# FFN gate and up products of a two-block kernel by Strassen's scheme, with summed weights kept in device memory

## The reference

```
def swiglu(h, w_gate, w_up, w_down):
    return (jax.nn.silu(h @ w_gate) * (h @ w_up)) @ w_down

# in first_block; D_FF is 2816
x_lat = x_lat + m_lat[2][:, None] * rms_norm(y_lat, norm_mix_post[layer])
f_lat = swiglu(modulate(rms_norm(x_lat, norm_ffn_pre[layer]), m_lat[3], m_lat[4]),
               w_gate[layer], w_up[layer], w_down[layer])
x_lat = x_lat + m_lat[5][:, None] * rms_norm(f_lat, norm_ffn_post[layer])
```

## Time and profile before

| | us |
|---|---|
| median of 3 runs | 3360.96 |
| lowest and highest | 3360.37, 3362.12 |
| time of the profiled execution | 3361.19 |
| its span in the profile | 3359.4 |
| PE busy (x instructions) | 3256.7 (x18179) |
| DVE, ACT, POOL busy | 1660.1, 1321.2, 252.8 |
| mean granted clock of PE | 0.988 |
| DMA | 328.24 MB, 98 GB/s in the mean |

### The profile page before, as it was taken

The page is one execution under the profiler, slowest core; times in us unless marked ns, Lnnn a source line. Parts: engine busy times, 40 slices in busy tenths (PEclk is TensorE's granted clock), DMA queues, the critical chain, the costliest instruction groups (busy, mean ns, idle before and its releaser), DMA issues.

```text
span 3359.4 us, 43733 instructions
## 1 busy us (share of the span) xinstructions
PE 3256.7 (97%) x18179; PEld 2585.9 (77%) x18179; DVE 1660.1 (49%) x2404; ACT 1321.2 (39%) x2266; POOL 252.8 (8%) x302
## 2 busy tenths in 40 slices
PE   6899888899999999999999999999999999999999
PEld 6677656787878878889955579999999555688887
DVE  6767576554343443345454553444434545534433
ACT  4532455454232333234445543333334455423322
POOL 1000313400000000000120000000000300000001
PEclk8999989999999999999999999999999999999999
DMA  6545213133333334333200112442432001124323
GB/s 246 167 156 164 82 44 114 58 127 112 120 115 96 97 94 170 94 94 118 88 1 7 51 48 89 132 131 85 149 128 85 6 7 51 47 88 134 108 94 113
DMA packets 97749, 328.24 MB, mean 98 GB/s; under 512 B 11456, under 2 KB 12880, under 8 KB 96784
## 3 DMA queue, kind: packets, MB, share of 16 engines
q1 hardware_dynamic: 77120, 252.55, 23.5%
q0 software_dynamic: 18896, 68.63, 5.9%
q10 hardware_dynamic: 1536, 4.26, 0.3%
HBM read 299.19 MB, written 26.21 MB: 97 GB/s over the span
## 4 chain that ended last, share of the span: by engine, by line
PE 90%; DVE 5%; ACT 2%; DMA 1%; issue 1%; ACTq 0%; DVEq 0%; POOL 0%; POOLq 0%
PE psum L146 88%; DVE mixer L175 2%; PE psum L149 2%; DVE mixer L185 1%; DVE wlo L175 1%; DMA mixer<-in_wm 1%; DVE junk L189 1%; DMA stage<-in_wi 0%; ACT whi L163 0%; DMA hold<-in_wq 0%; ACT arena L154 0%; ACT mixer L154 0%; ACT mixer L155 0%; DVE mixer L180 0%; ACT mixer L163 0%
## 5 line engine op out<-in xcount | busy, mean ns | idle before, releaser
L146 PE MATMUL psum<-region,whi 128*128 128x260 f32 (+2 forms) x7616 | 1831.6, 333 | 1.8 <-DVE region L185 1.8
L146 PEld LDWEIGHTS psum<-region,whi 128*128 128x128 f32 (+1 forms) x7616 | 1279.7, 186 | 164.5 <-DVE region L185 3.1
L146 PE MATMUL psum<-region,wlo 128*128 128x260 f32 (+2 forms) x3808 | 1265.8, 332 | 0.0
L175 DVE TENSOR_TENSOR wlo<-stage,whi 128x1024 fp32r<-128x1024 f32 (+2 forms) x454 | 510.3, 1126 | 677.3 <-ACT whi L163 676.6
L146 PEld LDWEIGHTS psum<-region,wlo 128*128 128x128 f32 (+1 forms) x3808 | 711.2, 187 | 78.4
L163 ACT CAST whi<-stage 128x1024 fp32r<-128x1024 f32 (+2 forms) x454 | 432.2, 968 | 214.2 <-PE psum L146 173.4
L154 ACT ACTIVATE arena<-psum 128x512 f32<-128x512 f32 (+2 forms) x412 | 193.2, 469 | 775.1 <-PE psum L146 771.9
L146 PE MATMUL psum<-arena 128*128 128x512 f32 (+11 forms) x1072 | 382.6, 480 | 1.9 <-ACT arena L154 1.4
L163 ACT COPY arena<-psum 128x260 f32<-128x260 f32 (+9 forms) x345 | 151.5, 444 | 402.4 <-PE psum L146 395.5
L175 DVE TENSOR_TENSOR arena<-arena,psum 128x512 f32<-128x512 f32 (+1 forms) x220 | 125.7, 572 | 327.3 <-PE psum L146 326.9
L175 DVE TENSOR_TENSOR arena<-arena 128x512 f32<-128x512 f32 (+8 forms) x341 | 204.5, 617 | 152.6 <-ACT arena L154 146.3
(11 more groups left out here) (166 smaller groups left out, 2677.6 us busy)
## 6 DMA issues: line engine op xcount, KB each, us to landing
stage<-in_w SPq DMA_DIRECT2D x144, 512.0 KB, 3.4
stage<-in_wi SPq DMA_DIRECT2D x55, 512.0 KB, 4.4
stage<-in_wo SPq DMA_DIRECT2D x48, 512.0 KB, 3.5
stage<-in_wg SPq DMA_DIRECT2D x44, 512.0 KB, 3.5
stage<-in_wu SPq DMA_DIRECT2D x44, 512.0 KB, 3.5
stage<-in_wm SPq DMA_DIRECT2D x42, 512.0 KB, 3.6
stage<-in_wd SPq DMA_DIRECT2D x32, 512.0 KB, 3.5
arena<-xr_scratch POOLq DMA_DIRECT2D x5, 2080.0 KB, 9.4
```

The lines of the kernel that those rows point to most:

```text
L146: return Issued(self, self.e and self.e.matmul(out, w, x, start=start, stop=stop, skip_group_check=True))
L175: return Issued(self, e and e.tensor_tensor(out, a, b, op))
```

## The change

**Gate and up.** The 22 groups become 11 pairs `j` of 256 hidden rows, and for each the product (weights 1024 x 256) by (input 1024 x 512) is made as a 2 x 2 block product by Strassen's scheme in the form with 7 products of blocks: hidden rows in halves of 128, k in halves of 512, tokens in halves of 256. Each product is 4 k-tiles x 3 matmuls of 256 columns. It needs four sums of weight blocks (T1 to T4, arrays `tg`, `tu` in device memory) and four of input blocks (s1 to s4). Three of the products are kept in SBUF by ACT (`m1`, `m5`, `m7`), and DVE assembles the four output blocks. Units of gate and up weights are 512 elements wide (256 KB), seven for each pair and matrix, and `stage`, `whi` and `wlo` are handed out in spots of 512 elements (6, 8 and 8). ACT and DVE work five units ahead. The parts are 4, 4 and 3 pairs; the down product is as before.

**The sums of weights** are made by POOL's transfers: for each of three parts 8 copies of weight blocks to `tg` and `tu` (1 MB, in the last part 0.75 MB), 6 adding transfers with another block, 4 adding T1 to T2 and T3's place: 54 in all, in the order `SUMS`. Twelve are issued in SSD, one a round; 14 in GLA, in every third round; 16 in the out projection, one after each result group; 12 in half 0 of the FFN. The first add of a part waits for all its copies, the first of the second kind for all of the first kind. SP waits for a part's last one before it loads from `tg`.

**Input of the FFN** (`Quarters` for `Halves`): ACT shifts each of 8 k-tiles in place, then seven blocks of 128 x 1024 elements are cast by ACT and made low by DVE, with four sums by DVE between.

**Norms** beside the out projection's results and the FFN are taken apart: DVE's sum, PE's product and ACT's inverse are steps of their own with empty steps between.

**Places in memory and loads** move accordingly: the second half's load of x for its last residual sum is issued behind the halving of the first in the next block's input.

```
@@ class Weights, sp_weights @@
+    def room(self, u):
+        out = [self.used(v) if self.seq[v][2] else self.lo[v] for v in self.sprev[u]]
+        if self.seq[u][0] in self.need:
+            count, step = self.need[self.seq[u][0]][self.seq[u][1] % 11]
+            out.append(count[step])
+        return out
...
-        if u >= W.NS:
-            v = u - W.NS
...
+        for f in W.room(u):
+            e.wait_ge(*f)
...
+PRODUCTS = (("M1", "11", "a11", "a"), ("M5", "T1", "s1", "c"), ("M7", "T3", "s3", "d"), ("M6", "T2", "s2", "b"),
+            ("M3", "22", "s4", "c"), ("M2", "21", "a12", "a"), ("M4", "T4", "a22", "d"))
+def pe_pair(e, W, bank, psum, key, name, j, h, done, A, leave, tick):
+    us = W.pair(key, name, j, done)
+    begun = {}
+    for n, (p, blk, x, b) in enumerate(PRODUCTS):
...
+        e.wait_ge(*h(x))
+        e.wait_ge(*W.hi[u])
+        e.wait_ge(*W.lo[u])
+        for k in range(kt):
+            e.matmul(o, wh[:, k, :], h.hi[x][:, k, :], b not in begun and k == 0, False)
+            e.matmul(o, wh[:, k, :], h.lo[x][:, k, :], False, False)
+            ins = e.matmul(o, wl[:, k, :], h.hi[x][:, k, :], False, k == kt - 1)
+        ins.then_inc(*done.up("unit", u))
...
+    (c0, f0, s0), (c1, f1, s1), (c2, f2, s2) = (sums_of_part(p) for p in range(3))
+    SUMS = c0 + c1[0:2] + f0 + c1[2:4] + s0 + c1[4:8] + c2[0:2] + f1 + c2[2:4] + s1 + c2[4:8] + f2 + s2
+    def weight_sum(e, n):
+        what, part, t, to, name, of = SUMS[n]
+        if what == "copy":
+            e.dma_start(block_of(t, to, part), block_of(name, of, part)).then_inc(*K.tcopy[part].up(t, to, by=16))
+        elif what == "first":
+            e.wait_ge(*K.tcopy[part]["tu", 3])
+            e.dma_start(block_of(t, to, part), block_of(name, of, part), accum_op=ALU.add).then_inc(
...
+        else:
+            e.wait_ge(*K.tfirst[part]["tu", 3])
...
@@ pool_ssd, each of 12 rounds @@
+            weight_sum(e, r)
@@ pool_gla, rounds of NL + 10 = 42 @@
+            if r % 3 == 1:
+                weight_sum(e, 12 + r // 3)
@@ Norm.steps @@
+        if gaps == ("apart",):
+            out += self.squares() + [("sum", self, 0)] + 2 * GAP + [("product", self, 0)] + GAP + [("inverse", self, 0)] + 2 * GAP
@@ Quarters @@
+    ACT_ORDER = ("a11", "a22", "a12", "s1", "s3", None, None, "s2", None, None, "s4")
+    DVE_ORDER = (("lo", "a11"), ("lo", "a22"), ("sum", "s1"), ("sum", "s3"), ("lo", "a12"), ("lo", "s1"), ("sum", "s2"),
+                 ("lo", "s3"), ("lo", "s2"), ("sum", "s4"), ("lo", "s4"))
...
+        return [("shift", self, k) for k in range(8)] + [("quarter", self, i) for i in range(11)]
@@ blocks @@
-    PARTS = ((0, 8), (8, 8), (16, 6))
+    PARTS = ((0, 4), (4, 4), (8, 3))
...
+    def ahead(key, n, last):
+        return W.pairs[key]["11"] + (min(n + 5, 8) if last else n + 5)
...
-                pe_gemm(e, W, bank, psum, ("wg", ch, k0 + k), "wg", [k0 + k],
-                        lambda ci, k_: (fh[:, k_], fl[:, k_], h(k_)), 1, 512, T, A)
-                bs.tick()
...
+                for name, leave in zip(("wg", "wu"), leaves(ch, j)):
+                    pe_pair(e, W, bank, psum, (name, ch, j), name, j, h, T, A, leave, tick)
@@ dve_ffn @@
+                        if p == "M4":
+                            e.wait_ge(*A[key, "m7"])
+                            e.tensor_tensor(m7, m1, m7, ALU.add, own=False).then_inc(*D.up(key, "V"))
...
+                            e.tensor_tensor(c21, o, m1, ALU.add, own=False).then_inc(*D.up(key, "C21"))
...
+                            e.tensor_tensor(c22, m5, m7, ALU.subtract, own=False).then_inc(*D.up(key, "C22"))
+                            if name == "wu":
...
+                                e.tensor_tensor(g[:, 256:1024], g[:, 256:1024], tu, ALU.mult).then_inc(*D.up("u", ch, j))
```

More of the change, by code:

```diff
@@ L258, in __init__ @@
         self.S, self.H, self.L, self.land, self.hi, self.lo, self.aps = S, H, L, land, hi, lo, aps
[L259 removed]
+        self.seq, self.spot, self.half, self.sprev, self.hprev = [], [], [], [], []
+        self.by, self.last, self.pairs, self.need = {}, {}, {}, {}
         self.rows = None
+        self.align(0, 0)
+        self.sown, self.hown = [None] * (2 * self.NS), [None] * (2 * self.NH)
         self.restart()
@@ L264, in restart, with align, place, take @@
         self.u = self.hi_u = self.lo_u = self.sp_u = 0
-    def take(self, key, name, i, raw, count, *step):
+    def align(self, spot, half):
+        self.next = [spot, half]
+    def place(self, which, own, size, width, u):
+        at = self.next[which] + (width == 2 and self.next[which] % 2)
+        at = 0 if at + width > size else at
+        self.next[which] = at + width
+        before = sorted({v for v in own[at:at + width] if v is not None})
+        own[at:at + width] = [u] * width
+        return at, before
+    def take(self, key, name, i, raw, count, *step, width=2):
         u = self.u
@@ L270, in take @@
             self.seq.append((name, i, raw))
-            self.half.append(self.count)
-            self.count += not raw
+            at, before = self.place(0, self.sown, 2 * self.NS, width, u)
+            self.spot.append(at)
+            self.sprev.append(before)
+            at, before = self.place(1, self.hown, 2 * self.NH, width, u) if not raw else (None, [])
+            self.half.append(at)
+            self.hprev.append(before)
         assert self.seq[u] == (name, i, raw)
@@ L276, in take, with pair @@
         return u
+    def pair(self, key, name, j, done):
+        t = "t" + name[1]
+        us = {}
+        for b, (n, kind) in BLOCKS.items():
+            us[b] = self.take((key, b), (name, t)[kind], 11 * n + j, False, done, "unit", self.u, width=1)
+        self.pairs[key] = us
+        return us
     def shape(self, u):
@@ L292, in used, with landed @@
         return count[step]
-    def half_before(self, u):
-        for v in range(u - 1, -1, -1):
-            if not self.seq[v][2] and self.half[v] == self.half[u] - self.NH:
-                return v
-        return None
+    def landed(self, u):
+        return self.land[self.spot[u]][u]
+    def room(self, u):
[4 more added lines that the diff above has]
+        return out
 def sp_weights(e, W, upto):
@@ new lines, in act_shift, with act_quarter @@
+def act_shift(e, h, k):
+    for c, s in h.ready(k):
+        e.wait_ge(*c[s])
+    e.activation(h.src[:, k], h.src[:, k], ACT.Identity, bias=h.B[:, k:k + 1], own=False).then_inc(
+        *h.st.act.up("shift", h.key, k))
+def act_quarter(e, h, i):
+    A, D, x = h.st.act, h.st.dve, h.ACT_ORDER[i]
+    if x is None:
+        return
+    e.wait_ge(*A["shift", h.key, 7 if x != "a11" else 3])
+    if i == 0:
+        for c, s in h.free:
+            e.wait_ge(*c[s])
+    if x in h.sums:
+        e.wait_ge(*D["sum", h.key, x])
+    e.copy(h.hi[x], h.at[x], own=False).then_inc(*A.up("hi", h.key, x))
@@ new lines, in dve_quarter @@
+def dve_quarter(e, h, i):
+    A, D = h.st.act, h.st.dve
+    what, x = h.DVE_ORDER[i]
+    e.wait_ge(*A["shift", h.key, 7 if i else 3])
+    if what == "lo":
+        if i == 0:
+            for c, s in h.free:
+                e.wait_ge(*c[s])
+        e.wait_ge(*A["hi", h.key, x])
+        e.tensor_tensor(h.lo[x], h.at[x], h.hi[x].bitcast(F32), ALU.subtract, own=False).then_inc(*D.up("lo", h.key, x))
+    else:
+        out, a, b, op = h.sums[x]
+        e.wait_ge(*A["hi", h.key, {"s1": "a22", "s3": "a11", "s2": "a11", "s4": "a12"}[x]])
+        for y in {"s2": ("s1",), "s4": ("s2",)}.get(x, ()):
+            e.wait_ge(*D["sum", h.key, y])
+        e.tensor_tensor(out, a, b, op, own=False).then_inc(*D.up("sum", h.key, x))
@@ L2192, in residual @@
     def residual(key, st, ch, col, dst, sq4, ready, free, by_two=None):
-        n = Norm((key, ch), st, yc[ch], 512, aff[:, col, :], yc[ch], sq4, rs2[:, 0:512], ready, free=free, by_two=by_two)
-        return n, n.steps() + [("add", (key, ch, dst, n), k) for k in range(8)] + [("store", (key, ch), 0)]
+        y = yc[key, ch]
+        n = Norm((key, ch), st, y, 512, aff[:, col, :], y, sq4, rs2[:, 0:512], ready, free=free, by_two=by_two)
+        return n, n.steps("apart") + [("add", (key, ch, dst, n), k) for k in range(8)] + [("store", (key, ch), 0)]
     def added(n, key, ch, dst, nxt):
@@ L2424, in act_ffn @@
                 key = ("wd", ch, part, m)
-                act_weights(e, W, W.last[key] + 2)
+                act_weights(e, W, ahead_down(key, m))
                 if part == 0:
                     e.wait_ge(*T[key, 0])
-                    e.copy(yc[ch][:, m], psum[:, bank.of[key, 0], :], own=False).then_inc(*A.up(key, 0))
-                bs.tick(2 if part == 2 else 1)
+                    e.wait_ge(*(sffn.dve["add", ("end", 0), m] if ch else sout.dve["add", ("post", 1), m]))
+                    e.copy(yd[:, m], psum[:, bank.of[key, 0], :], own=False).then_inc(*A.up(key, 0))
@@ L3560, in build @@
         K.late = sig("mod_rows")
```

(4 more changed lines are left out.)

357 lines of the change are left out of this document (250 added, 107 removed).

## The result

The changed kernel takes 3372.1 us (median of 7 runs, 3366.9 to 3375.3), the kernel before 3361.0 (median of 7). The ratio is 1.003, 95% interval 1.0018 to 1.0042: slower by 0.3%, where 0.8% faster was forecast. The profiled execution took 3366.9 us with a span of 3365.0.

The account below looks back on a forecast made before the run. The prediction took PE's instructions to bound the kernel, provided DVE, ACT and the transfers keep up. Its sum was 3361.2 - 49.3 + 11.3 + 3 + 2 + 5 = 3333 us, range 3322 to 3364.

Parts of the forecast that it names:

- What bounds the kernel: Whole kernel, FFN above all: PE instructions set the time; removing them pays in full if DVE, ACT and transfers keep up.
- Gate and up: FFN's gate and up products: 3696 matmuls of 256 columns at 0.120 us replace 2112 of 512 at 0.2333, -49.3 us.
- The start of half 0: FFN's beginning: PE waits for shifts, casts, lows and sums of the input, net +11.3 us, bounds +7 and +16.
- Steady state: FFN's pairs of products: DVE and ACT work is covered by PE's, cost 0, upper bound 8 us.
- Ends of parts: FFN, before each down product: PE waits for the last pair's low half, +3 us, bounds 1 and 8.
- The loads: FFN weight loads: six spots give a 256 KB load 8.6 us, it needs 2.7, so free.
- POOL's issues: GLA rounds: 14 transfers issued between POOL's products at 0.75 us each, +2 us, bounds 0 and 10.5.
- The wait at transfer 18: GLA, POOL's round 19: POOL waits for six adds of 7 us each, and PE for POOL, +5 us.
- Norms apart: Norms beside the FFN: split steps take DVE's sum out of PE's wait, at most 1.6 us, taken as 0.
- (a): Adds of 13 us: POOL's wait stalls GLA 40 us, 3368; second batch holds POOL in out projection, 3388; chance 0.20.
- (b) to (d): DVE or wait order bounds the FFN: 3355, chance 0.17; POOL's issues on GLA's path: 3342; cheap start, free adds: 3324, 0.08.

Follow-up runs that it names:

- e1: The changed kernel with all 54 transfers of the weight sums left out, loads reading the plain weights instead; 3325.0 us, ratio 0.9891.
- e5: The changed kernel with adds and copies in 2 KB pieces and the 54 transfers issued earlier, none in the FFN; 3338.1 us, ratio 0.9926.
- e2: The changed kernel with the same 54 transfers cut in 2 KB pieces, instead of 8 KB for adds and 64 KB for copies; 3351.9 us, ratio 0.9976.
- e4: The changed kernel with the three norms beside the FFN put back in one step each; 3379.0 us, ratio 1.005.

## Why the prediction was wrong, point by point

**What bounds the kernel**: the FFN by its PE instructions, right; "as long as the transfers keep up" was the condition, and it failed.

**Gate and up**, -49.3 us: right in kind, mis-sized. The new matmuls are spaced 0.1167 us, not 0.120: in e1, 40 triples from 785.86 to 799.86, 14.00/120 (the timeline shows each triple as a pair and a single).

```profile
785.86 0.40 PE L153 MATMUL psum<-region,whi 128*128 128x256 f32 x2
...
799.86 0.40 PE L153 MATMUL psum<-region,whi 128*128 128x256 f32 x2
```

So 3696 x 0.1167 = 431 us and the term is -61.5. A single triple of 256 columns and a run of 260 were too thin a base; 512 columns at 0.2333 halve exactly.

**The start of half 0**, +11.3: right. (Its own parts, 15.2 + 1 - 4.7, make 11.5.) In e1, whose fillers stand 2.57 us later than before's, M1 begins at 772.06 (forecast 769.7 + 2.6), M5 at 777.79 (775.5 + 2.6), and M3 at 784.74; with M3, M2 and M4 of 1.4 us each the pair ends near 789.0 (786.8 + 2.6). From the first filler that is 24.9 us, of which 9.8 are matmuls, so 15.1 are lost; before lost 4.9 (10.5 less 5.6). The term is +10.2. In the changed kernel 9.9 us more are lost there, 15.95 against 6.05, by late loads.

**Steady state**, 0 with 8 as the bound: B to C is 40.3 us shorter in e1 than before, and -40.3 = -61.5 + 10.2 + 5.6 (part ends) + 1.6 (the product at C) + x, so x is 3.8 us. The timeline shows 1.4 of them as waits (0.52, 0.67 and 0.23 us); the rest is not placed. DVE did not bound it.

**Ends of parts**, +3: e1 waits 1.97, 1.45, 0.71 and 1.45 us there, 5.6, within the bounds. The two of 1.45 are the ends of the parts of three pairs, forecast at 1.4 each; the other two end parts of four, which were to lose nothing.

**The loads**, "Free": **this is the step that failed.** The step took the loads as covered by six spots and five units of lead. It was worked out from a load's 2.7 us in the kernel before and the loads' own 182 GB/s. It left out that twelve transfers of the sums and their backlog run beside the same FFN, on the same 16 engines: beside them a load of 256 KB took 19.5 us to land, against the 8.6 us that six spots give it, and ACT waited 47 us for weights from 762 to 905. By e1, that and the late start cost B to C 746.1 - 714.2 = 32 us, and e5, with all transfers ahead of the FFN, has 713.4.

**POOL's issues**, +2: no row shows them on the path, and e2, with all of them, takes 687.3 us from A to B, e1 without any 687.4.

**The wait at transfer 18**, +5 (its own numbers give 55.3 - 49 - 2 = 4.3): the price of 7 us an add is near for one that is alone (7.8 us to landing, with 71% of all engines for 7.9 us, so 5.6 us of them all), the mechanism isn't right. I counted the loads of 560 to 585 as work ahead of the adds, and not the adds as work ahead of the loads. 14.0 us were lost by a load that PE needed, and not by a wait of POOL's. From A to B the transfers cost 700.9 - 687.4 = 13.5 us.

**Norms apart**, 0: too low. The bound of 1.6 us was PE's idle time in an FFN where DVE was 41% busy. With the new FFN's DVE work behind, the joined norms wait 5.4, 5.9 and 2.3 us (e4), and the split saves about 7 of it. What a part of a change is worth has to be read beside the other parts.

**Rivals**: (a) had the right sign and the wrong place. It named the adds' price and POOL's wait; the loss came from the adds' packets in the loads' way. Its second half did happen: the second batch held POOL for 27.95 us in the out projection, and the store of half 0 with it, but PE is not seen to wait for that. (b) to (d) did not happen. Without the transfers the forecast of all else, 3333 - 5 - 2 = 3326, is 1 us from e1, which is luck, for its errors cancel. The matmuls gave 12.2 us more and the start 1.1; the steady state, the part ends and the product at C took 8.0 more. In e1 A to B is 3.0 us longer than before and C to the end 2.7, for which I have no cause.

## What to carry to other kernels

A transfer "in the background" has a price even when nobody waits for it: list the loads that are in flight beside it, and for each the slack of the engine that it feeds. Adding transfers in the background belong in pieces no larger than those of the loads they run beside (some 20 us here; the size of the copies' pieces made no difference, 0.9976 against 0.9977). They belong where DMA engines are idle, not where SP's loads run only five units ahead. A wait of a transfer in an engine's queue needs as much distance as the transfers take in the crowd (16 to 26 us here), not alone (7.8).

## What the runs showed of the hardware

- An adding transfer of 1024 KB from device memory to device memory alone lands in 7.8 us and fills 71% of the 16 engines meanwhile; a plain copy of that size lands in 5.2 to 5.7 us; in the crowd the adds' medians are 20 and 26 us. From 617.3 to 625.2 in the changed kernel, the queue of the adds (packets, MB, share), and the landing of the add that is alone there:

```profile
q0 software_dynamic: 144, 1.05, 71.0%
...
tg_scratch<-tg_scratch POOLq DMA_DIRECT2D x2, 1024.0 KB, 7.8
```

- Against adds in 8 KB pieces the loads' queue moves packets one for one (381 and 381 in 15 us), 52 GB/s; with 2 KB pieces the counts are equal again (477 and 474 in 10 us of e2) and it moves 162 GB/s over those 15 us. Against copies with their large pieces it isn't one for one (693 to 72).
- Matmuls of 256 columns are spaced 0.1167 us in these products, half of 512's 0.2333.
